# Block inverses in a delta-rule mixer: whole-array transposes instead of identity products

## The reference, cut to what matters

```
diff = gc[..., :, None] - gc[..., None, :]
decay = jnp.where(incl, jnp.exp(jnp.where(incl, diff, 0.0)), 0.0)
kb = kc * bc
lower = jnp.where(strict, jnp.einsum("bhnid,bhnjd->bhnij", kb, kc) * decay, 0.0)
a_mat = lower + jnp.eye(C, dtype=F32)
rhs = jnp.concatenate([vc * bc, kb * jnp.exp(gc)[..., None]], axis=-1)
sol = lax.linalg.triangular_solve(a_mat, rhs, left_side=True, lower=True, unit_diagonal=True)
```

## Time and profile before

| | |
|---|---|
| median of three runs | 642.76 us (642.0 to 643.0) |
| span of the profiled execution, first to last instruction | 640.4 us |
| median time less that span | 2.4 us |
| PE, DVE, ACT, POOL busy | 91%, 39%, 31%, 26% of the span |
| mean granted clock of PE | 0.986 |

### The profile page before, as it was taken

How to read it: one execution, slowest core, us unless ns; L and a number is a source line. 1 busy time by engine, 2 the same in 40 slices (tenths; PEclk the granted TensorE clock), 3 DMA queues, 4 the chain that set the end, 5 groups by cost and what they waited for, 6 DMA issues and landing times.

```text
span 640.4 us, 12045 instructions
## 1 busy us (share of the span) xinstructions
PE 582.7 (91%) x4942; PEld 453.3 (71%) x4942; DVE 251.9 (39%) x630; ACT 198.4 (31%) x429; POOL 169.0 (26%) x112
## 2 busy tenths in 40 slices
PE   4999999999998999999999999999999988887881
PEld 3997887899998888777779988665665655454430
DVE  5225453681226522457772154333233322221127
ACT  6444444622333162434534331121111111011123
POOL 1344334272458322300123401111211121110011
PEclk9999999999999999989999999999999999999996
DMA  8755443322212111000069999999999999999983
GB/s 324 221 154 182 140 139 101 115 68 68 58 45 67 35 44 58 1 2 2 1 151 407 409 396 400 372 415 422 418 419 420 418 420 419 420 421 418 415 339 148
DMA packets 49910, 151.63 MB, mean 237 GB/s; under 512 B 8495, under 2 KB 29823, under 8 KB 37440
## 3 DMA queue, kind: packets, MB, share of 16 engines
q1 hardware_dynamic: 45232, 142.69, 58.2%
q0 software_dynamic: 4560, 8.15, 3.4%
q10 hardware_dynamic: 64, 0.02, 0.0%
HBM read 142.70 MB, written 16.27 MB: 248 GB/s over the span
## 4 chain that ended last, share of the span: by engine, by line
PE 58%; SPq 12%; DVE 9%; DMA 7%; issue 4%; POOL 4%; ACT 1%; POOLq 0%; ACTq 0%; DVEq 0%
PE bank L719 26%; PE bank L743 7%; SPq L608 5%; DMA w<-in_expert_w_dram 5%; PE bank L1091 4%; PE bank L1056 4%; PE bank L1071 4%; SPq L611 4%; SPq L614 3%; PE bank L1011 2%; PE bank L883 1%; PE bank L1025 1%; DMA yt<-yd 1%; DMA yd<-oy,dst 1%; PE bank L1005 1%
## 5 line engine op out<-in xcount | busy, mean ns | idle before, releaser
L1399 POOL TENSOR_TENSOR wlo<-raw,whi 128x1024 fp32r<-128x1024 f32 (+1 forms) x38 | 91.0, 2396 | 178.5 <-ACT whi L1112 178.5
L719 PE MATMUL bank<-whi,hHi 128*128 128x256 f32 (+2 forms) x320 | 97.3, 304 | 3.2 <-DVE cacc L1573 1.4
L719 PE MATMUL bank<-whi,hLo 128*128 128x256 f32 (+2 forms) x320 | 94.2, 294 | 0.0
L719 PE MATMUL bank<-wlo,hHi 128*128 128x256 f32 (+2 forms) x320 | 94.1, 294 | 0.0
L1112 ACT ACTIVATE whi<-raw 128x1024 fp32r<-128x1024 f32 (+1 forms) x38 | 40.3, 1061 | 94.1 <-PE bank L719 83.9
L1056 PE MATMUL bank<-w,xT 128*64 128x256 f32 x512 | 60.0, 388 | 8.9 <-issue 6.7
L719 PEld LDWEIGHTS bank<-whi,hHi 128*128 128x128 f32 x320 | 60.8, 190 | 6.7 <-DVE hLo L1818 2.1
L1071 PE MATMUL bank<-w,xT 128*64 128x256 f32 x512 | 58.3, 380 | 5.8 <-DMA w<-in_expert_w_dram 5.8
L1056 PEld LDWEIGHTS bank<-w,xT 128*64 128x64 f32 x512 | 39.2, 140 | 34.1 <-issue 17.6
L719 PEld LDWEIGHTS bank<-whi,hLo 128*128 128x128 f32 x320 | 60.8, 190 | 1.4
L719 PEld LDWEIGHTS bank<-wlo,hHi 128*128 128x128 f32 x320 | 60.9, 190 | 1.1
(11 more groups left out here) (335 smaller groups left out, 910.3 us busy)
## 6 DMA issues: line engine op xcount, KB each, us to landing
w<-in_expert_w_dram SPq DMA_DIRECT2D x47, 2048.0 KB, 27.3
raw<-in_w_in_dram SPq DMA_DIRECT2D x24, 512.0 KB, 3.7
yd<-zt SPq DMA_DIRECT2D x8, 512.0 KB, 5.2
raw<-in_w_out_dram SPq DMA_DIRECT2D x8, 512.0 KB, 4.3
yt<-yd SPq DMA_DIRECT2D x4, 1024.0 KB, 9.0
raw<-in_w_in_dram SPq DMA_DIRECT2D x6, 520.0 KB, 7.6
X<-in_x_dram SPq DMA_DIRECT2D x4, 512.0 KB, 7.0
x<-in_x_dram SPq DMA_DIRECT2D x4, 512.0 KB, 5.8
```

The source lines that it names most:

```text
L719: m = pe.matmul(o, l, r, start=(at == 0 and c == 0 and i == 0), stop=(at == parts - 1 and kc == chunks[-1] and i == 2), skip_group_check=True)
L1399: pool.tensor_tensor(part(wlo[g % 2], g), part(raw[g % 3], g), part(whi[g % 2], g).bitcast(F32), ALU.subtract).then_inc(wlo_done, 1)
```

## The change

`XT` and, in levels 1 to 4, `UT` become two whole-array transposes a tile (`turned_pairs`), each of 128 columns, two heads at once. Transposing 128x128 moves a block from one partition half to the other for half of the heads, so `Uc` and `Yc` get a crossed layout, and every other block product of `Y` and `Xp` reads one partition half and writes the other (`crossed`). The products that stay in their half come first for both tiles; those that cross wait until that tile's first group is finished (`diag_done`). `UT` now stands ahead of `Y`. `bB` becomes a transpose too. DVE builds `Yc` in four pieces instead of two. Level 5 is as before.

```diff
-                b += [("Y", 2 * pr, lv), ("Y", 2 * pr + 1, lv)]
-                if lv:
-                    b += [("UT", 2 * pr, lv), ("UT", 2 * pr + 1, lv)]
+                y, u = ([(n, 2 * pr, lv), (n, 2 * pr + 1, lv)] for n in ("Y", "UT"))
+                b += y if lv == 0 else y + u if lv == LEVELS - 1 else u + y
...
+            def crossed(names, f, to_rows):
+
+                def some(i, across):
+                    for q in range(NH // 2):
+                        for b in range(2):
+                            e = 1 - b if across else b
+                            h, u = 2 * q + e, 2 * q + b
+                            ps = psum(names[i])
+                            o = ps[HALVES[b], h * HB:(h + 1) * HB] if to_rows else ps[HALVES[e], u * HB:(u + 1) * HB]
+                            m = f(i, h, u, HALVES[b], HALVES[e], o)
+                    return m
+
+                for i in range(2):
+                    begin(names[i])
+                    some(i, False).then_inc(diag_done, 1)
+                for i in range(2):
+                    diagonals[0] += 1
+                    pe.wait_ge(diag_done, diagonals[0])
+                    end(some(i, True), names[i])
+
+            def turned_pairs(name, a):
+                ps = begin(name)
+                for q in range(NH // 2):
+                    m = pe.transpose(ps[:, q * P:(q + 1) * P], a[:, 2 * q:2 * q + 2, :].rearrange("p b n -> p (b n)"), ident)
+                end(m, name)
...
-                    four(("bB", t), lambda h, o: mm(o, br[:, 4 * t + h:4 * t + h + 1].broadcast_to([P, P]), ident))
+                    four(("bB", t), lambda h, o: pe.transpose(o, br[:, 4 * t + h:4 * t + h + 1].broadcast_to([P, P]), ident))
...
-                        blocks(("XT", t), lambda h, r, o: mm(o, Uc[t % 2][r, h, :], id64[r, :]))
+                        turned_pairs(("XT", t), Uc[t % 2])
...
-                        if lv < LEVELS - 1:
-                            blocks(("Y", t, lv), lambda h, r, o: mm(o, Nm[i][r, h, r], Xc[i][r, h, :]))
-                        else:
+                        if lv == LEVELS - 1:
                             blocks(("Y", t, lv), lambda h, r, o: mm(o, Nm[i][UP, h, DN], Xc[i][UP, h, :]), (DN,))
-                    if lv:
-
-                        for i in range(2):
-                            blocks(("UT", 2 * pr + i, lv), lambda h, r, o: mm(o, Xc[i][r, h, :], id64[r, :]))
+                        elif lv:
+                            turned_pairs(("UT", t, lv), Xc[i])
+                    for i in range(2):
+                        t = 2 * pr + i
+                        if lv == LEVELS - 1:
+                            blocks(("UT", t, lv), lambda h, r, o: mm(o, Xc[i][r, h, :], id64[r, :]))
+                    if lv < LEVELS - 1:
+                        crossed([("Y", 2 * pr + i, lv) for i in range(2)],
+                                lambda i, h, u, b, e, o: mm(o, Nm[i][b, h, b], Xc[i][b, h, :]), False)
                     for i in range(2):
                         t = 2 * pr + i
                         wait_read(pe, ("Y", t, lv))
                         if lv:
                             wait_read(pe, ("UT", t, lv))
-                        if lv < LEVELS - 1:
-                            blocks(("Xp", t, lv), lambda h, r, o: mm(o, Uc[i][r, h, :], Yc[i][r, h, :]))
-                        else:
+                        if lv == LEVELS - 1:
                             blocks(("Up", t, lv), lambda h, r, o: mm(o, Yc[i][DN, h, :], Um[i][DN, h, DN]), (UP,))
+                    if lv < LEVELS - 1:
+                        crossed([("Xp", 2 * pr + i, lv) for i in range(2)],
+                                lambda i, h, u, b, e, o: mm(o, Uc[i][e, u, :], Yc[i][e, u, :]), True)
...
-                    half = lambda m, r: m[r, :].unsqueeze(1).broadcast_to([HB, NH, HB])
-                    dve.tensor_tensor(Yc[i][UP, :, :], Nm[i][UP, :, UP], half(const("nM1"), UP), ALU.mult)
-                    link(dve.tensor_tensor(Yc[i][DN, :, :], Nm[i][DN, :, DN], half(const("nM1"), DN), ALU.mult))
+                    for e, to in enumerate((UP, DN)):
+                        for c, r in enumerate((UP, DN)):
+                            j = dve.tensor_tensor(Yc[i][to, c::2, :], Nm[i][r, e::2, r],
+                                                  const("nM1")[r, :].unsqueeze(1).broadcast_to([HB, NH // 2, HB]), ALU.mult)
+                    link(j)
```

More of the change, by code:

```diff
@@ L392, in build @@
         y_copied = sem("y_copied")
-        rot_done = sem("rot_done")
+        rot_done = sem("rot_done"); diag_done = sem("diag_done")
         sx_ready = sem("sx_ready"); pe_ready = sem("pe_ready"); pf_ready = sem("pf_ready"); foxh_done = sem("foxh_done")
@@ L743, in mm @@
                 return pe.matmul(o, l, r, start=True, stop=True)
+            HALVES = (UP, DN)
+            diagonals = [0]
+            def crossed(names, f, to_rows):
[20 more added lines that the diff above has]
+                end(m, name)
             def task(k):
```

## The result

The changed kernel takes **652.24 us** (median of 4 runs, 649.58 to 655.02); the kernel before took 642.88 beside it (642.0 to 643.62). The ratio on record, over all runs of both, is 1.016 [1.013, 1.019]; the two medians by themselves give 1.0146. It is slower by some 9.4 us, where 4.8 were forecast, and 0.7 us above the upper end of the range. The profiled execution is the longest of the four: span 653.1, its own time 655.02. So its trace explains 12.7 us of span, of which a typical run has about three quarters.

What follows compares the result with a forecast made beforehand. PE's chain was taken to bound the stage at 129 to 263 us. Levels 1 to 4 (1.5 + 1.4) plus XT and level 0 (0.7 + 1.2) gave +4.8 on 642.8: 647.6 us, range 641.5 to 651.5.

Steps and rivals of the forecast that it cites:

- Starting 0.45 earlier, the four pieces fit ahead of 135.35 and only one operation waits: Pair 0, ahead of level 0: shorter bB starts DVE's chain 0.45 us earlier, so its pieces mostly precede POOL's products.
- this escape: DVE's earlier start in pair 0 makes XT of tile 1 punctual: +0.7 us there, +1.2 if it fails.
- rival D: Longer gaps and transposes bring on three falls of PE's clock, at most 1.5 us each, ending above 651.5; chance 0.03.
- The levels: Levels 1 to 4: lost mask cover and late ACT copies add 1.5 us in pair 0, 1.4 in pair 1.
- Levels 2 and 4 of pair 1: ACT gates Xp in level 2, +0.30 us; level 4 is followed at once by level 5, +0.50.
- The stream of a crossed batch: Y and Xp batches with crossing products: 0.97 us from first to last start instead of 0.93, waits nearly hidden.
- rival A: Each crossing group waits for the array to run empty and restarts: +7 to +10 us, about 651; chance 0.13.
- The gap ahead of Xp in pair 0: Between Y's last start and Xp's first, PE stands idle about 1.0 us while DVE masks.
- `bB`'s saving in tiles 2 and 3: Pair 1: transposes save 0.45 us a tile, but PE then waits in KK, so nothing arrives.
- Pair 1's XT and level 0: Level 0 adds 0.68 us and the turn before it 0.5, together +1.2.
- Rivals B and C: B: PE's saved work counts, mask does not, about 640.0, chance 0.11. C: existing stalls absorb half or more, 642 to 644, 0.15.

Runs made afterwards that it cites:

- e2: The kernel before with only bB made by transposes, as in the change: 641.42 us, ratio 1.0012.
- e3: The changed kernel with POOL's gate products of both tiles held back until DVE's uinit, so DVE's pieces meet no product: 645.71 us, ratio 1.0083.
- e7: The kernel before with Yc in four pieces and bB by transposes, both together: 645.21 us, ratio 1.0071.
- e14: The changed kernel with POOL's low part of granules 20 and 27 made to wait for DVE's uinit: 648.79 us, ratio 1.0127.
- e4: The changed kernel with throwaway identity products on PE ahead of its wait for DVE (17 in pair 0, 6 in pair 1): 648.23 us, ratio 1.0120.
- e8: The changed kernel with bB made by products again: 650.10 us, ratio 1.0148.
- e9: The changed kernel with POOL's gate products held back and the first tile's Y and Xp issued on its own reads: 642.26 us, ratio 1.0013.
- e10: The changed kernel with POOL's gate products held back and UT behind Y again: 647.94 us, ratio 1.0105.
- e12: e9 with ACT copying XT and UT before it splits the next weights, in nine places: 640.23 us, ratio 0.9974.
- e1: The kernel before with only Yc built in four pieces, layout left as it was: 641.85 us, ratio 1.0015.

## Why the forecast fell short

**What failed first: "Starting 0.45 earlier, the four pieces fit ahead of 135.35 and only one operation waits. Then XT of tile 1 is no longer late".** There was no free time ahead of POOL's products. POOL's low part runs from 130.73 to 135.41 and holds DVE's first piece, which began at 134.575, took 0.97 instead of 0.27 and ended at 135.55, 0.14 behind the low part. So the second began at 135.561, behind POOL's product at 135.36, and took 1.29; so did the third. The four took 3.88 and not 1.1 to 2. An earlier start only makes that first operation wait longer: in e2, where nothing but `bB` differs from before, L1700 takes 1.08 us instead of 0.77 and ends 0.28 behind the low part in both. In e3, e7 and e14 too the first piece ends 0.14 to 0.15 behind it. Nor did the chain start 0.45 earlier: its first operation moved from 131.86 to 131.77, since DVE itself was busy until 131.55. The trace of before had the sign, in a row that I hadn't taken into the earlier trace rows: L1700 took 0.77 for tile 0 and 0.40 for tile 1. My 135.35 stands in no row; POOL's products start at 135.12 there.

```profile
130.47 4.68 POOL L1399 TENSOR_TENSOR wlo<-raw,whi 128x1024 fp32r<-128x1024 f32 x2
134.66 0.77 DVE L1700 TENSOR_TENSOR Ym<-Nm,CT 64x256 f32<-64x256 f32 x1
141.00 0.40 DVE L1700 TENSOR_TENSOR Ym<-Nm,CT 64x256 f32<-64x256 f32 x1
```

I gave the failure of this escape a price of 0.5 us ("it is +1.2"), by adding up DVE's own times, and didn't ask whom the late DVE meets next. It meets POOL's low part, which now starts 0.19 us ahead of it, where it started 0.83 behind in before, and pays 2.0 more. A first lateness was counted; the second meeting with POOL was not. e7 shows this pair of causes without the rest of the change, e14 that mending the race alone gives back 3.6 us in its stage. Without the race and with the clock whole the stage of pair 0 is still +2.0 (e14), not +1.2.

**What failed second: the clock, put at nothing in the sum and at 0.03 in rival D.** As a size D was near, "at most 1.5 us each" for three falls: with PE kept busy through the same lateness, e4 gives back 1.5 + 1.6 us in pair 0 and 0.9 in pair 1, and its stage is 4.2 us shorter. But these come from one fall of 10.2 us and one of 3.4. I took the length of a fall from the one fall I had looked at the earlier trace rows as if every fall had it (my window held 3.0 of its 3.4 us), and didn't tie the chance to a long idle gap, which follows from the first mistake. The transposes are not a cause that the runs support: e3 and e4 have every transpose of the change and run at 1.00 from 125 to 275 us.

**A term too small.** The levels come to +3.4 us for 2.9. Levels 2 and 4 of pair 1 are +0.48 and +0.87 for 0.30 and 0.50: ACT's copies gate Xp there, with 1.32 and 1.47 us from Y's last start. The second profile of the change and e3 have 1.32 in both, and 3.3 for the levels.

**What held.** The stream of a crossed batch, 0.98 for 0.97: rival A is refuted, the other tile's records do hide the wait. The gap ahead of Xp in pair 0, 1.0 to 1.1 for 1.0, and with it the 3.85 and 3.75 of pair 0's levels. `bB`'s saving in tiles 2 and 3: that stretch takes 8.15 us in both kernels, and KK's wait grows from 1.1 to 2.04. Pair 1's XT and level 0 are +1.0 in e3, with the clock whole, for 1.2 (the working takes 0.45 ahead of Y and the sum 0.5). Together e3 gives 5.2 us for the 4.8 of the sum. Rivals B and C are refuted by e3 as well: the cover was needed, and nothing absorbed the delay.

**What stays open.** Why the clock falls in pair 1 of e8 and e14 for 6.8 us, in e9 and e10 for 3.4, and in e3, e4 and e12 not at all, wasn't settled. The size of the gaps doesn't decide it: e3 and e10 both have PE idle for 1.86 and 0.67 us there, and only e10 has a fall; e8 and e14 have 1.1 to 1.2, 0.52 and 0.67 and the longest falls, while the change starts with 1.16 and 0.52 and falls for 3.4. Nor is it known why the fall in pair 0 lasts 10.2 us behind 3.71 us of idle PE in the change, and 3.4 us behind 3.30 in e7. So the clock's share differs from run to run, and the stages of single profiles don't order e8 and e14 as the medians do. That DVE's operation was held by POOL's, and not by something that coincides with it, is shown by the order of starts in the profiles (held, 2.45 to 2.48, in both of the change, e4 and e7; not held, 0.42 to 0.43, in before, e1, e2, e8 and, by an edit of the order alone, e14). No run gave this operation other operands; what speaks for the operands is that DVE's operations on PSUM beside the same work of POOL keep their time.

## What to carry to other kernels

When an edit delays one engine or speeds up another, redo the timeline around every operation that shares a port with theirs: in this kernel 0.2 us of order decided over 2 us. Then look at who stands idle behind it. Count work that "only" fills an engine's queue as the cover that it is, and when it goes, make each consumer wait for its own tile's operands alone. Price a long idle gap on TensorE in a busy stretch with a fall of the clock on top: here 3.71 us of gap brought some 3 us of it in the gap's own stage and the next.

## What the runs showed of the hardware

- DVE's product of two SBUF operands against POOL's of 128x1024: started 0.15 us earlier it takes 0.43 us (e1), started 0.18 to 0.19 later 2.45 to 2.46 (e7, after), ending 0.29 us behind POOL's. A piece of 64x128 takes 0.27 to 0.29 alone and 1.29 behind a product of 1.34. DVE's operations that read a PSUM bank (L1725, 1.12 for four) take the same beside POOL's low part and without it. The Trainium skill, SBUF — State Buffer, SBUF: two separate sides, calls this pair of ports a lock and not a split of bandwidth; the trace agrees.
- TensorE's clock stayed at 1.2 GHz for 10.2 us after a gap of 3.71 us, though PE was back at work 1.25 us into it (fall at 144.1, XT at 145.35). In e7 it stayed there for 3.4 us after a gap of 3.30, and fell only when PE was back at work for 1.2 us (145.3, XT at 144.07). With 17 products of no use in the same gap (e4) it stayed at 2.4 GHz throughout.
- Batches in which two quarters of the array read one partition half and write the other are streamed at nearly the rate of the others, 0.98 us for 32 records against 0.93, with a wait for the tile's own first group in each.
